# A decoder-trunk kernel on one core: 32x32 diagonal blocks inverted on VectorE, two doubling levels left on TensorE

## The chip, the core and the metric

The kernel runs on one core of a Trainium2 chip. The metric is the device time in microseconds (us) of one execution; lower is better. All tensors are float32.

## What is computed

One layer of a hybrid decoder on 256 tokens of width 1024: a combined projection, a gated-DeltaNet head group (4 heads) and a differential-attention head group (4 heads), their output projection and a layer norm; then cross attention to 256 memory tokens and a layer norm; then a mixture of experts (top 4 of 32) and a last layer norm. The change touches the gated-DeltaNet part alone. The reference solves, per chunk and head, a unit lower triangular system:

```python
lmat = jnp.where(strict, jnp.einsum('bhncd,bhnsd->bhncs', k_beta, k) * decay, 0.0)
amat = lmat + jnp.eye(C)
rhs = jnp.concatenate([v_beta, k_beta * jnp.exp(g)[..., None]], -1)
sol = lax.linalg.triangular_solve(amat, rhs, left_side=True, lower=True, unit_diagonal=True)
```

## The kernel before

It is written out by hand: each engine has its own straight list of instructions, and semaphores order them. The gated-DeltaNet part works on 8 pairs (2 blocks of 128 tokens by 4 heads; `PAIRS`), so there are 8 triangular matrices `I + L` of 128x128. TensorE fills one PSUM bank at a time; each filling is a unit with a name (`dqk0`, `LT0`, `M1_0` ...). The list `UNITS` gives their order, eight banks are used in turn, and column "A" or "D" of the list says whether ScalarE (ACT) or VectorE (DVE) empties the bank. A unit begins when the unit eight places before it has been emptied.

**The inverses.** `X` holds the inverse of each triangular matrix so far and `XT` its transpose, both 128x1024 (8 pairs of 128 columns). Blocks of size 1 are their own inverse, the first level (blocks of 2) is written straight from the mask and `L`: DVE does it for `X` (L1426 and L1428), GpSimd (POOL) for `XT` (L513 and L515) after ACT has emptied `LT0` and `LT1`, the transposes of `L`. Six levels follow (`for level in range(1, LEVELS)`), each of which doubles the block size: POOL masks `LT` into `BT` (L521); TensorE makes `M = BT' X` (L959, units `M{level}_0` and `_1`), ACT empties it (L575), TensorE makes the products for `X` (L964) and for `XT` (L966), and DVE subtracts them (L1471 and L1473). The last level makes `XT` alone.

**What fills the waits.** Behind each level TensorE has other work that depends on nothing in it (`LEVEL_FILL`): `dqk3` behind level 1 (L818), `dv0` behind 2 (L828), `dv1` and four transposes `memT` behind 3 (L828, L810), and behind levels 4, 5 and 6 the scores of differential head 0, 1 or 2 (`sc`, L939) and one quarter of the memory keys (`km`, L818). Behind levels 5 and 6 also `aT`, the transposed attention (L948). The softmax of a head goes DVE `shifted` (L1444 to L1449), ACT `diff_exp` (L660), DVE `combine` (L1455 to L1462), TensorE `attention_T`.

**After the levels** come the products that use the inverse (`U`, `WT`, `S`, `O0`, `WS`, `O1`), head 3 of the differential attention, `vm0`, `OD0`, `OD1`, `vm1`, the mixing projection, cross attention, and the expert loop: 33 rounds, in each of which a block of up to 64 tokens goes through one expert (one of the 32 experts has two blocks). An expert's weights come in six loads of 2 MB. SyncE (SP) issues the weight loads; the buffers hold two experts, and a load waits until TensorE has used the part that it overwrites (L435).

```python
            pool.tensor_tensor(XT, LT, tile_b(levT[0], PAIRS, P), ALU.mult)
            pool.drain()
            pool.tensor_tensor(XT, tile_b(ident, PAIRS, P), XT, ALU.subtract).then_inc(xt_init, 1)
...
            tt(X, L, tile_b(lev0, PAIRS, P), ALU.mult)
            dve.drain()
            tt(X, tile_b(ident, PAIRS, P), X, ALU.subtract).then_inc(x_init, 1)
```

Of the kernel before, what the change touches and what calls it, by code (L numbers as in the profile page):

```python
# [26 lines left out]
P = 128  # L27
# [16 lines left out]
LEVELS = 7  # L44
DIFF_D = 64
# [16 lines left out]
K_ID, K_IOTA, K_UT, K_US, K_ONE, K_CM, K_LEV0, K_LEVT = 0, 128, 192, 320, 448, 576, 960, 1088  # L62
N_CONST = K_LEV0
N_LEVEL_MASKS = P * (LEVELS + 1)
K_END = K_LEV0 + N_LEVEL_MASKS


def constants():

    r = np.arange(P)[:, None]  # L70
    c = np.arange(P)[None, :]
    out = np.zeros((P, K_END), np.float32)
    out[:, K_ID:K_ID + P] = r == c
    out[:, K_UT:K_UT + P] = r <= c
    out[:, K_US:K_US + P] = r < c
    out[:, K_ONE:K_ONE + P] = 1.0
    future = np.where(c > r, NEG, 0.0)
# [7 lines left out]
    out[:, K_LEV0:K_LEV0 + P] = below(r, c, 1)  # L85
    for level in range(LEVELS):
        at = K_LEVT + P * level
        out[:, at:at + P] = below(c, r, 1 << level)
    return out
# [13 lines left out]
def unit_table():  # L103
# [7 lines left out]
    u += [("LT0", "A"), ("LT1", "A"), ("dqk2", "A")]  # L111
# [7 lines left out]
    u += [("U0", "A"), ("U1", "A"), ("WT", "A"), ("sc3_0", "D"), ("sc3_1", "D"), ("S", "A"), ("O0", "A"), ("aT2", "A")]  # L119
    u += [("WS", "D"), ("km3", "A"), ("O1", "A"), ("aT3", "A"), ("vm0", "A"), ("OD0", "A"), ("OD1", "A"), ("vm1", "A")]  # L120
# [54 lines left out]
def trunk_kernel(nc, d, out):  # L175
    ctx = ExitStack()
    with ctx:
# [77 lines left out]
        lev0 = ln_mem[:, 0:P]  # L255
        levT = [ln_mem[:, P * (1 + i):P * (2 + i)] for i in range(LEVELS)]
# [115 lines left out]
        lmat_ready = sem("lmat_ready")  # L372
        x_init = sem("x_init")
# [119 lines left out]
        def _(pool):  # L493
# [15 lines left out]

            wait_emptied(pool, "LT1")  # L510
            wait_emptied(pool, "KQ1")
            pool.wait_ge(ld_lev, 16)
            pool.tensor_tensor(XT, LT, tile_b(levT[0], PAIRS, P), ALU.mult)  # L513
            pool.drain()
            pool.tensor_tensor(XT, tile_b(ident, PAIRS, P), XT, ALU.subtract).then_inc(xt_init, 1)  # L515
            for level in range(1, LEVELS):
                if level == 1:
# [33 lines left out]
        def _(act):  # L551
# [9 lines left out]
            act.dma_start(ln_mem[:, 0:N_LEVEL_MASKS], d["consts"][:, K_LEV0:K_LEV0 + N_LEVEL_MASKS]).then_inc(ld_lev, 16)  # L561
# [73 lines left out]
            empty("dqk2", dqk3[:, 4:6, :], as3(2))  # L635

# [38 lines left out]
            for level in range(1, LEVELS):  # L675
                for g in range(TB):
                    empty(f"M{level}_{g}", M1[:, 4 * g:4 * g + 4, :], as3(4))
                if level == 1:
                    empty("dqk3", dqk3[:, 6:8, :], as3(2))
                elif level <= 3:  # L680
                    empty(f"dv{level - 2}", dv3[:, level - 2, :])
                if level == 3:
                    for i in range(4):
                        empty_T("memT", i, memT)
                if level >= 4:
                    diff_exp(level - 4, 0)
                    diff_exp(level - 4, 1)
                    empty_km(level - 4)
                    if level > 4:
                        empty_aT(level - 5)  # L690
# [4 lines left out]
            empty_head_out("O0", o_flat[:, 0:512], 0, 0, 0)  # L695
            empty_aT(2)
            diff_exp(3, 0)
            diff_exp(3, 1)
            empty_km(3)
            empty_head_out("O1", o_flat[:, 512:1024], 1, 1, 0)  # L700
# [87 lines left out]
        def _(pe):  # L788
# [162 lines left out]

            pe.wait_ge(x_init, 1)
            pe.wait_ge(xt_init, 1)
            for level in range(1, LEVELS):
                pe.wait_ge(bt_ready, level)
                for g in range(TB):
                    if level > 1:
                        need(f"X{level - 1}_{g}", f"XT{level - 1}_{g}")
                    per_head(f"M{level}_{g}", lambda o, h: pe.matmul(o, BT[:, 4 * g + h, :], X[:, 4 * g + h, :],  # L959
                                                                   start=True, stop=True))  # L960
                for g in range(TB):
# [6 lines left out]
                if level == 1:  # L968
                    dqk_unit(3)
                elif level == 2:  # L970
                    arrived(6)
                    dv_unit(0)
                    used_up(2, "dqk3")
                elif level == 3:
                    dv_unit(1)
                    pe.wait_ge(ld_mem, 16)
                    for i in range(4):
                        transpose_block(f"memT{i}", mem3[:, i // 2, :], range(4 * (i % 2), 4 * (i % 2) + 4))
                else:
                    if level == 4:  # L980
                        need("memT3", "dqk3")
                        used_up(1, "dv1")
                        arrived(7)
                        arrived(8)
                    scores(level - 4)
                    km_unit(level - 4)
                    if level > 4:
                        attention_T(level - 5)
# [6 lines left out]
            scores(3)  # L995
# [4 lines left out]
            attention_T(2)  # L1000
            need("WT", "S")
            per_head("WS", lambda o, h: pe.matmul(o, wT[:, h, :], S_sb[:, h, :], start=True, stop=True))
            km_unit(3)
# [5 lines left out]
            last.then_inc(unit_filled, 1)  # L1009
            attention_T(3)  # L1010
# [297 lines left out]
        def _(dve):  # L1308
# [117 lines left out]
            tt(X, L, tile_b(lev0, PAIRS, P), ALU.mult)  # L1426
            dve.drain()
            tt(X, tile_b(ident, PAIRS, P), X, ALU.subtract).then_inc(x_init, 1)  # L1428
            dve.wait_ge(xt_init, 1)
# [36 lines left out]
            for level in range(1, LEVELS):  # L1466
# [8 lines left out]
                if level >= 4:  # L1475
                    if level > 4:
                        combine(level - 5)
                    shifted(level - 4, 0)
                    shifted(level - 4, 1)
# [20 lines left out]
            combine(2)  # L1500
            shifted(3, 0)
            shifted(3, 1)
# [4 lines left out]
            dve.sem_inc(dve_emptied, 1)  # L1507
            combine(3)
# [253 lines left out]
```

## Time and profile before

| what | value |
|---|---|
| median of 3 runs | 1304.68 us (1303.6 to 1306.26) |
| the profiled execution | 1308.02 us |
| its span (first to last instruction) | 1306.3 us |
| mean granted TensorE clock | 0.985 |
| TensorE matmul busy | 1256.5 us (96%) |
| VectorE / ScalarE / GpSimd busy | 331.2 / 282.8 / 46.6 us |
| moved by DMA | 446.83 MB, mean 342 GB/s |

The span is the profiled execution without the 1.7 us that lie around it. A busy engine is not yet the bound: the chain of waits says which work ended last at each point of time, and the timeline says what an engine waited for before an instruction. Times in rows are microseconds from the span's start. PE is TensorE. A full-width fp32 product stands in the rows as two instructions; the built order below counts it as one.

### The profile page before, as it was taken

How to read it: one execution, taken by the hardware profiler on the slowest of the kernel's cores; microseconds unless marked ns; L12 is line 12 of the kernel's file. 1: busy time of each engine (PE TensorE's matmuls, PEld its weight loads, DVE VectorE, ACT ScalarE, POOL GpSimd, SP SyncE). 2: the span in 40 equal slices, each digit the busy share in tenths (PEclk: the TensorE clock that was granted, in tenths of full speed). 3: DMA queues.
4: the chain of work that ended last, by engine and by line, in shares of the span. 5: the costliest groups of instructions: out<-in, count | busy, mean ns of one | idle time of the engine just before them, and what ended most of it. 6: DMA issues, size and time to landing. Idle time of an engine off the chain costs nothing.

```text
span 1306.3 us, 15882 instructions
## 1 busy us (share of the span) xinstructions
PE 1256.5 (96%) x5875; PEld 589.3 (45%) x5876; DVE 331.2 (25%) x935; ACT 282.8 (22%) x501; POOL 46.6 (4%) x39
## 2 busy tenths in 40 slices
PE   7999999999989999999999999999999999998994
PEld 6878796685533333333333333333333333333331
DVE  1652252320421122211222112221112212111115
ACT  0231233111112122121221212212122211221121
POOL 0103101000100000000000000000000000000001
PEclk9999999999889999999999999999999999999998
DMA  8650404058769994999999999999999999999992
GB/s 312 229 208 7 189 1 169 35 227 335 303 264 426 430 427 180 429 427 430 427 430 428 427 429 428 428 429 427 429 428 428 429 428 429 428 428 429 428 429 85
DMA packets 42903, 446.83 MB, mean 342 GB/s; under 512 B 6768, under 2 KB 7104, under 8 KB 18304
## 3 DMA queue, kind: packets, MB, share of 16 engines
q1 hardware_dynamic: 39312, 441.50, 80.5%
q10 hardware_dynamic: 3568, 5.01, 1.2%
q8 instruction: 16, 0.26, 0.1%
q14 instruction: 7, 0.06, 0.0%
HBM read 445.44 MB, written 1.05 MB: 342 GB/s over the span
## 4 chain that ended last, share of the span: by engine, by line
PE 77%; DMA 19%; issue 2%; DVE 1%; POOL 0%; another core or an unknown queue 0%; SPq 0%; POOLq 0%; ACT 0%; DVEq 0%; ACTq 0%
PE bank L1240 28%; DMA main<-in_exp_w_up_dram 19%; PE bank L1283 13%; PE bank L828 8%; PE bank L818 5%; PE bank L1213 3%; PE bank L1181 3%; PE bank L1255 3%; PE bank L1047 2%; PE bank L1187 1%; PE bank L869 1%; PE bank L959 1%; PE bank L966 1%; PE bank L859 1%; PE bank L964 1%
## 5 line engine op out<-in xcount | busy, mean ns | idle before, releaser
L1240 PE MATMUL bank<-main 128*64 128x512 f32 x2112 | 478.4, 604 | 20.9 <-DMA main<-in_exp_w_up_dram 16.3
L1240 PEld LDWEIGHTS bank<-main 128*64 128x64 f32 x2112 | 154.5, 139 | 313.7 <-issue 309.7
L1283 PE MATMUL bank<-main,kst 128*64 128x512 f32 x1056 | 241.1, 598 | 0.0
L1691 DVE TENSOR_TENSOR main<-bank,main 128x256 f32<-128x256 f32 x66 | 28.1, 425 | 588.2 <-PE bank L1255 588.2
L772 ACT ACTIVATE main<-bank 128x512 f32<-128x512 f32 x66 | 39.4, 597 | 430.5 <-PE bank L1240 430.5
L1283 PEld LDWEIGHTS bank<-main,kst 128*64 128x64 f32 x1056 | 69.9, 136 | 122.9 <-issue 118.6
L828 PE MATMUL bank<-main 128*128 128x512 f32 x256 | 111.9, 592 | 0.3 <-ACT main L648 0.3
L818 PE MATMUL bank<-main 128*128 128x256 f32 x352 | 77.9, 380 | 0.0
L828 PEld LDWEIGHTS bank<-main 128*128 128x128 f32 x256 | 47.9, 190 | 56.1 <-issue 55.9
L818 PEld LDWEIGHTS bank<-main 128*128 128x128 f32 x352 | 66.3, 190 | 10.2 <-issue 1.5
L1213 PE MATMUL bank<-main 64*128 64x512 f32 x272 | 67.6, 615 | 0.7 <-ACT main L781 0.7
L575 ACT ACTIVATE main<-bank 128x512 f32<-128x512 f32 (+2 forms) x59 | 33.9, 587 | 155.4 <-PE bank L818 54.9
L1181 PE MATMUL bank<-main,kst 128*64 128x512 f32 x272 | 65.6, 604 | 1.2 <-issue 1.2
L1255 PEld LDWEIGHTS bank<-kst,main 128*128 128x128 f32 x264 | 36.8, 209 | 53.5 <-issue 53.5
L1255 PE MATMUL bank<-kst,main 128*128 128x128 f32 x264 | 49.3, 309 | 0.0
L526 POOL TENSOR_TENSOR small<-small 128x1 f32<-128x1 f32 (+1 forms) x10 | 8.4, 837 | 1101.6 <-DVE small L1717 944.9
L779 ACT ACTIVATE main<-bank 128x256 f32<-128x256 f32 x33 | 12.7, 386 | 151.6 <-PE bank L1292 151.6
L1678 DVE TENSOR_SCALAR main<-kst,small 128x128 f32<-128x128 f32 x66 | 15.9, 284 | 108.4 <-PE bank L1292 105.6
L772 ACT ACT_TABLE_LOAD x33 | 42.3, 1283 | 3.5 <-DVEq L1664 2.9
L781 ACT ACTIVATE main<-bank 128x512 f32<-128x512 f32 x33 | 19.7, 597 | 105.9 <-PE bank L1283 105.9
L777 ACT ACT_TABLE_LOAD x33 | 42.3, 1283 | 0.6
L1181 PEld LDWEIGHTS bank<-main,kst 128*64 128x64 f32 x272 | 19.8, 138 | 40.0 <-issue 40.0
(247 smaller groups left out, 855.1 us busy)
## 6 DMA issues: line engine op xcount, KB each, us to landing
main<-in_exp_w_gate_dram SPq DMA_DIRECT2D x64, 2048.0 KB, 30.1
main<-in_exp_w_up_dram SPq DMA_DIRECT2D x64, 2048.0 KB, 34.5
main<-in_exp_w_down_dram SPq DMA_DIRECT2D x64, 2048.0 KB, 32.9
main<-in_w_in_dram SPq DMA_DIRECT2D x7, 2048.0 KB, 27.8
main<-in_xa_wk_dram SPq DMA_DIRECT2D x2, 2048.0 KB, 10.9
main<-in_w_out_dram SPq DMA_DIRECT2D x2, 2048.0 KB, 11.3
main<-in_xa_wv_dram SPq DMA_DIRECT2D x2, 2048.0 KB, 10.7
main<-in_xa_wq_dram SPq DMA_DIRECT2D x2, 2048.0 KB, 13.2
```

The costliest lines, as they stand in the source:

```text
L575: act.activation(dst, ps[:, :] if src is None else src(ps), func, **kw).then_inc(act_emptied, 1)
L772: act.activation(gu[:, f, :], gu_bank[f][:, :], ACT.Copy).then_inc(gu_copied, 1)
L777: act.activation(sig[:, f, :, :], mg[:, f, :, :], ACT.Sigmoid, scale=SWIGLU_ALPHA).then_inc(sig_ready, 1)
L818: last = pe.matmul(ps[:, j * SEQ:(j + 1) * SEQ], w(k)[:, c * P:(c + 1) * P], src[:, k, :], start=(k == 0), stop=(k == KC - 1))
L828: last = pe.matmul(ps[:, :], srcT[:, k, b * P:(b + 1) * P], w(k)[:, col:col + 512], start=(k == 0), stop=(k == KC - 1))
L1047: last = pe.matmul(ps[:, j * SEQ + b * P:j * SEQ + (b + 1) * P], w(k)[:, (2 * i + j) * P:(2 * i + j + 1) * P], xT[:, k, b * P:(b + 1) * P] ...
L1181: last = pe.matmul(ps[64 * h:64 * h + 64, :], selw[:, b, 0:CAP], x3[:, b, h * HALF:(h + 1) * HALF], start=(b == 0), stop=(b == 1))
L1213: last = pe.matmul(acc[b][h][:, :], gselT[64 * h:64 * h + 64, b * P:(b + 1) * P], y_sb[64 * h:64 * h + 64, :], start=False, stop=final)
L1240: last = pe.matmul(gu_bank[f][64 * side:64 * side + 64, :], xg_chunk(k), weights(role, k, f), start=(k == 0), stop=(k == KC - 1))
L1255: last = pe.transpose(guT_bank[f][:, j * P:(j + 1) * P], gu[:, f, :].rearrange("p (c j) -> p j c", j=4)[:, j, :], ident)
L1283: last = pe.matmul(y_bank[64 * h:64 * h + 64, :], hT[:, k, :], weights(role, k, h), start=(k == 0), stop=(k == KC - 1))
L1691: tt(mg[:, f, :, :], gT[:, :, 0, :], bias(0), ALU.add)
```

## The change

Levels 1 to 4 and the two masked first steps go. In their place the 32 diagonal blocks of 32x32 (4 in each of the 8 pairs) are inverted together on DVE. POOL writes `diag`, the diagonal blocks of `I - L`, in four instructions of 32 partitions each. A DVE transpose in 32x32 blocks spreads them over the partitions as `factor`: a partition then holds one whole block and solves 8 of its 32 columns, so four partitions share a block. Row `r` of the inverse is a product of `r + 1` factors with 8 columns of the rows so far, summed: one multiply and one reduction, 31 times, each waiting for the one before. Two transposes and two masked copies then write `X` and `XT`. TensorE goes on at level 5. The fillings are placed anew: `dqk3`, `dv0` and `memT` ahead of level 5, the scores and `dv1` behind it, head 1, `km0` and `aT0` behind level 6, and the rest (`km1`, `km2`, heads 2 and 3) among the products that use the inverse. The load of the masks shrinks from 1024 to 516 columns.

```diff
+FIRST_LEVEL = 5
...
 LEVEL_FILL = {
-    1: [("dqk3", "A")],
-    2: [("dv0", "A")],
-    3: [("dv1", "A")] + [(f"memT{i}", "A") for i in range(4)],
-    4: [("sc0_0", "D"), ("sc0_1", "D"), ("km0", "A")],
-    5: [("sc1_0", "D"), ("sc1_1", "D"), ("km1", "A"), ("aT0", "A")],
-    6: [("sc2_0", "D"), ("sc2_1", "D"), ("km2", "A"), ("aT1", "A")],
+    5: [("sc0_0", "D"), ("sc0_1", "D"), ("dv1", "A")],
+    6: [("sc1_0", "D"), ("sc1_1", "D"), ("km0", "A"), ("aT0", "A")],
 }
...
+            pool.wait_ge(lmat_ready, 2)
+            pool.wait_ge(unit_filled, UNIT_AT["ktok1"] + 1)
+            for q in range(4):
+                rows = slice(32 * q, 32 * q + 32)
+                pool.drain()
+                last = pool.tensor_tensor(diag[rows, :, :], ident[rows, rows].unsqueeze(1).broadcast_to([32, PAIRS, 32]),
+                                          L[rows, :, rows], ALU.subtract)
+            last.then_inc(diag_ready, 1)
...
+            dve.wait_ge(diag_ready, 1)
+            dve.transpose(factor, diag.rearrange("p g k -> p k g").unsqueeze(3).broadcast_to([P, 32, PAIRS, 4]))
+            dve.drain()
+            for r in range(1, 32):
+                done = solved[:, 0:r + 1, :].rearrange("p k j -> p j k")
+                product = products[:, 0:8 * (r + 1)].rearrange("p (j k) -> p j k", j=8)
+                tt(product, factor[:, 0:r + 1, r].unsqueeze(1).broadcast_to([P, 8, r + 1]), done, ALU.mult)
+                dve.drain()
+                dve.reduce_sum(solved[:, r, :], product, AX_X)
+                dve.drain()
...
+            dve.transpose(diag_X.rearrange("p g (d j) -> p j g d", j=8), solved.rearrange("p r j -> p j r"))
+            dve.drain()
+            spread(X, diag_X).then_inc(x_init, 1)
+            dve.transpose(diag_XT, diag_X)
+            dve.drain()
+            spread(XT, diag_XT).then_inc(xt_init, 1)
...
-            for level in range(1, LEVELS):
+            for level in range(FIRST_LEVEL, LEVELS):
                 for g in range(TB):
                     empty(f"M{level}_{g}", M1[:, 4 * g:4 * g + 4, :], as3(4))
...
+                if level == FIRST_LEVEL:
+                    empty("dv1", dv3[:, 1, :])
+                    diff_exp(0, 0)
+                    diff_exp(0, 1)
+                else:
+                    empty_km(0)
+                    empty_aT(0)
+                    diff_exp(1, 0)
+                    diff_exp(1, 1)
```

TensorE's queue from the filling ahead of the first level on, before (the names in these rows are regions of memory: `main` is SBUF, `kst` the constants, `bank` PSUM):

```order
L818 MATMUL bank<-main 128x256 x16
L959 MATMUL bank<-main 128x128 x8
L964 MATMUL bank<-main 128x128 x4
L966 MATMUL bank<-main 128x128 x4
L964 MATMUL bank<-main 128x128 x4
L966 MATMUL bank<-main 128x128 x4
L818 MATMUL bank<-main 128x256 x16
L959 MATMUL bank<-main 128x128 x8
```

And now, from `dqk2` and `dqk3` on (L836 here is L818 before, L846 is L828, L828 is L810, L984, L990 and L992 are L959, L964 and L966):

```order
L836 MATMUL bank<-main 128x256 x32
L846 MATMUL bank<-main 128x512 x8
L828 MATMUL bank<-kst,main 128x128 x16
L984 MATMUL bank<-main 128x128 x8
L990 MATMUL bank<-main 128x128 x4
L992 MATMUL bank<-main 128x128 x4
L990 MATMUL bank<-main 128x128 x4
L992 MATMUL bank<-main 128x128 x4
L957 MATMUL bank<-main 128x128 x2
L957 MATMUL bank<-main 128x256 x2
L846 MATMUL bank<-main 128x512 x8
L984 MATMUL bank<-main 128x128 x8
```

Three fillings now stand in one piece ahead of the first level, and behind level 5 only the scores and `dv1` stand ahead of the `M` of level 6.

ACT's queue, before, at the end of level 4 and in level 5 (behind the last of `memT` come `M4_0` and `M4_1`, the exponentials of head 0, then `km0`, `M5_0`, `M5_1`):

```order
L648 ACTIVATE main<-bank 128x4x128 x4
L575 ACTIVATE main<-bank 128x512 x2
L660 ACTIVATE main,small<-main,small 128x128
L660 ACTIVATE main,small<-main,small 128x256
L660 ACTIVATE main,small<-main,small 128x128
L660 ACTIVATE main,small<-main,small 128x256
L575 ACTIVATE main<-bank 128x512 x3
```

And now (L663 is L648 before, L588 is L575, L675 is L660; the three behind `memT` are `M5_0`, `M5_1` and `dv1`, the three behind the exponentials `M6_0`, `M6_1` and `km0`):

```order
L663 ACTIVATE main<-bank 128x4x128 x4
L588 ACTIVATE main<-bank 128x512 x3
L675 ACTIVATE main,small<-main,small 128x128
L675 ACTIVATE main,small<-main,small 128x256
L675 ACTIVATE main,small<-main,small 128x128
L675 ACTIVATE main,small<-main,small 128x256
L588 ACTIVATE main<-bank 128x512 x3
```

The exponentials of head 0 stood ahead of the emptying of the filling behind their level; they now stand behind it, directly ahead of `M6_0`.

## Rows read from the trace of the kernel before

**Rows 1.** The page: TensorE's busy time, and the chain's shares by engine.
```profile
PE 1256.5 (96%) x5875; PEld 589.3 (45%) x5876; DVE 331.2 (25%) x935; ACT 282.8 (22%) x501; POOL 46.6 (4%) x39
...
PE 77%; DMA 19%; issue 2%; DVE 1%; POOL 0%; another core or an unknown queue 0%; SPq 0%; POOLq 0%; ACT 0%; DVEq 0%; ACTq 0%
```

**Rows 2.** The chain of waits, 110 to 150 us: start us, us, what.
```profile
110.85 2.02 PE bank L959 x16
112.87 0.95 PE bank L964 x8
113.82 0.89 PE bank L966 x8
...
123.41 1.78 PE bank L959 x16
...
147.98 1.75 PE bank L810 x16
```

**Rows 3.** SP's queue in the timeline: start us, us from first to last issue.
```profile
472.08 4.29 SPq L435 DMA_DIRECT2D main<-in_exp_w_down_dram  x2
510.16 0.34 SPq L435 DMA_DIRECT2D main<-in_exp_w_gate_dram  x1
```

**Rows 4.** Busy time by stretch; the last three columns: granted clock, DMA share, GB/s.
```profile
363.00:366.00 3.00, 2.77 (x8) 0.93 (x10) 1.23 (x6) 0.05 (x1) 0.00 (x0) 0.50 0.02 5
...
495.00:500.00 5.00, 5.00 (x26) 1.89 (x27) 1.70 (x5) 0.39 (x1) 0.00 (x0) 1.00 0.00 0
```

**Rows 5.** PE's timeline, 93 to 111 us: start us, us, work, idle before.
```profile
93.80 1.04 PE L926 MATMUL bank<-kst,main 128*128 128x128 f32 x8
...
102.45 7.07 PE L818 MATMUL bank<-main 128*128 128x256 f32 x32
110.85 1.35 PE L959 MATMUL bank<-main 128*128 128x128 f32 x10 [1.32 <-POOL main L521]
```

**Rows 6.** DVE's timeline, 352 us on: small instructions, each after a drain.
```profile
352.00 0.23 DVE L1617 TENSOR_TENSOR small<-small 128x64 f32<-128x64 f32 x1
352.30 0.22 DVE L1619 TENSOR_REDUCE small<-small 128x2 f32<-128x64 f32 x1
```

**Rows 7.** One group by line: count, then busy us and mean ns.
```profile
L1343 DVE COPY main<-small 128x1024 f32<-128x1024 f32 x1 | 0.7, 696 | 0.1
```

**Rows 8.** Timeline of DVE and POOL, 97 to 111 us.
```profile
98.46 1.23 DVE L1428 TENSOR_TENSOR main<-kst,main 128x1024 f32<-128x1024 f32 x1
108.39 2.21 DVE L1433 TENSOR_TENSOR small<-small 128x1 f32<-128x1 f32 x1 [8.71 <-POOL main L515]
...
103.44 2.35 POOL L513 TENSOR_TENSOR main<-main 128x1024 f32<-128x1024 f32 x1 [12.42 <-ACT main L575]
105.93 2.35 POOL L515 TENSOR_TENSOR main<-kst,main 128x1024 f32<-128x1024 f32 x1
108.24 2.35 POOL L521 TENSOR_TENSOR main<-main 128x1024 f32<-128x1024 f32 x1
```

**Rows 9.** ACT's timeline: an emptying ahead of another, and one head's exponentials.
```profile
148.02 0.60 ACT L575 ACTIVATE main<-bank 128x512 f32<-128x512 f32 x1 [9.90 <-PE bank L828]
148.51 2.06 ACT L648 ACTIVATE main<-bank 128x512 f32<-128x512 f32 x4
...
196.15 0.44 ACT L660 ACTIVATE main<-main,small 128x128 f32<-128x128 f32 x1
...
197.81 0.22 ACT L660 ACTIVATION_READ_ACCUMULATOR main<-main,small 128x1 f32 x1
```

**Rows 10.** The chain: eight transposes of dense columns, four of every fourth column.
```profile
243.75 0.87 PE bank L810 x8
...
406.71 0.68 PE bank L1255 x4
```

**Rows 11.** The chain: the first and the third round's weight products.
```profile
363.23 15.02 PE bank L1240 x56
...
421.79 12.02 PE bank L1240 x56
```

More of the change, by code:

```diff
@@ L110, in unit_table @@
     u += [("KK0", "D"), ("KK1", "D"), ("KQ0", "D"), ("KQ1", "D"), ("ktok0", "D"), ("ktok1", "D"), ("dqk1", "A")]
-    u += [("LT0", "A"), ("LT1", "A"), ("dqk2", "A")]
-    for level in range(1, LEVELS):
+    u += [("LT0", "A"), ("LT1", "A"), ("dqk2", "A"), ("dqk3", "A"), ("dv0", "A")] + [(f"memT{i}", "A") for i in range(4)]
+    for level in range(FIRST_LEVEL, LEVELS):
         u += [(f"M{level}_0", "A"), (f"M{level}_1", "A")]
@@ L254, in trunk_kernel @@
         iota = kst[:, K_IOTA:K_IOTA + CAP]
-        lev0 = ln_mem[:, 0:P]
-        levT = [ln_mem[:, P * (1 + i):P * (2 + i)] for i in range(LEVELS)]
+        levT = {level: ln_mem[:, S_LEVT + P * i:S_LEVT + P * (i + 1)] for i, level in enumerate(range(FIRST_LEVEL, LEVELS))}
+        block_mask = ln_mem[:, S_BLOCK:S_BLOCK + 4]
+        solved = ln_mem[:, S_EYE:S_EYE + 256].rearrange("p (r j) -> p r j", j=8)
+        factor = conv_out[:, 0:1024].rearrange("p (k r) -> p k r", k=32)
+        products = conv_out[:, 1024:1280]
+        diag, diag_X, diag_XT = (conv_out[:, 256 * i:256 * (i + 1)].rearrange("p (g c) -> p g c", g=PAIRS) for i in (5, 6, 7))
         ln_g, ln_b = ln_mem[:, 0:D_MODEL], ln_mem[:, D_MODEL:2 * D_MODEL]
@@ L635, in _ @@
             empty("dqk2", dqk3[:, 4:6, :], as3(2))
+            empty("dqk3", dqk3[:, 6:8, :], as3(2))
+            empty("dv0", dv3[:, 0, :])
             def empty_km(i):
@@ L949, in attention_T @@
                 last.then_inc(unit_filled, 1)
+            dqk_unit(3)
+            arrived(6)
+            dv_unit(0)
+            used_up(2, "dqk3")
+            pe.wait_ge(ld_mem, 16)
+            for i in range(4):
+                transpose_block(f"memT{i}", mem3[:, i // 2, :], range(4 * (i % 2), 4 * (i % 2) + 4))
             pe.wait_ge(x_init, 1)
-            pe.wait_ge(xt_init, 1)
-            for level in range(1, LEVELS):
-                pe.wait_ge(bt_ready, level)
+            for level in range(FIRST_LEVEL, LEVELS):
+                pe.wait_ge(bt_ready, level - FIRST_LEVEL + 1)
                 for g in range(TB):
-                    if level > 1:
+                    if level > FIRST_LEVEL:
                         need(f"X{level - 1}_{g}", f"XT{level - 1}_{g}")
@@ L967, in _ @@
                                                                     start=True, stop=True))
[L968 to L974, printed above, removed]
+                if level == FIRST_LEVEL:
+                    need("dqk3")
+                    scores(0)
                     dv_unit(1)
-                    pe.wait_ge(ld_mem, 16)
-                    for i in range(4):
-                        transpose_block(f"memT{i}", mem3[:, i // 2, :], range(4 * (i % 2), 4 * (i % 2) + 4))
-                else:
[L980 to L988, printed above, removed]
+                else:
+                    scores(1)
+                    need("memT3")
+                    arrived(7)
+                    arrived(8)
+                    km_unit(0)
+                    attention_T(0)
+                    used_up(1, "dv1")
             for g in range(TB):
@@ L994, in _ @@
             per_head("WT", lambda o, h: pe.matmul(o, kbg[:, 4 + h, :], XT[:, 4 + h, :], start=True, stop=True))
-            scores(3)
+            scores(2)
             need("U0")
@@ L1464, in combine @@
                 last.then_inc(a_ready, 1)
-            for level in range(1, LEVELS):
+            for level in range(FIRST_LEVEL, LEVELS):
                 for g in range(TB):
@@ L1474, in _ @@
                 dve.drain()
[L1475 to L1479, printed above, removed]
+                if level > FIRST_LEVEL:
+                    combine(0)
+                shifted(level - FIRST_LEVEL, 0)
+                shifted(level - FIRST_LEVEL, 1)
             roots = [0]
@@ L1507, in _ @@
             dve.sem_inc(dve_emptied, 1)
+            combine(2)
+            shifted(3, 0)
+            shifted(3, 1)
             combine(3)
```

78 lines of the change are left out of this document (39 added, 39 removed).

## The prediction

> **What bounds the kernel now.** First the page: TensorE is busy for 96% of the span, but the chain gives it 77% and gives 19% to DMA [rows 1], so two stretches with different bounds must be told apart. The chain in order of time does that. From 110.85 us on it steps from one TensorE group straight to the next through all six levels [rows 2]; there the time is TensorE's, and a product taken away is time gained, as long as nothing else comes late. DMA ends the chain in the last quarter, in the expert loop. So the second question is whether a gain made at 110 us survives the loads. SP's queue answers it. In the round in which one expert has a second block, SP issues its last load at about 476 us and the next at 510.16 [rows 3], and the engines moved nothing between 495 and 500 us [rows 4]. That pause ends when TensorE frees a buffer. Before it, DMA stood idle at 363 to 366 us [rows 4], again until TensorE frees the first one. The load stream behind each pause therefore starts at a time that TensorE sets. All of it moves when TensorE is earlier, and the end with it. I pass the gain on in full.
>
> **What goes from TensorE.** A level is one group of `M` and four of `X`, `XT`: in level 1, 2.02 + 0.95 + 3 x 0.89 = 5.64 us, in level 2 with 1.78 in front 5.40 us, in levels 3 and 4 the same within 0.01 [rows 2]. Four levels: 5.64 + 3 x 5.40 = 21.84 us. The first `M` after a wait costs 2.02 instead of 1.78, and that now falls on level 5: -0.24. The old wait ahead of level 1, 1.32 us for POOL's `XT` and `BT`, goes [rows 5]: +1.32. With no new wait the gain would be 22.9 us. The other units are all still there, only moved.
>
> **What now has to be ready, and when.** TensorE starts `dqk2` at 102.45 us [rows 5], as before. Behind it stand `dqk3` (a unit like it), `dv0` and `memT`. `dqk2` and `dqk3` take 6.9 us each, `memT` 1.75 [rows 2], `dv0`, eight 512-column products, also 6.9 as its work is that of `dqk2`. TensorE is through at about 102.45 + 3 x 6.9 + 1.75 = 124.9 us. The question is whether `X` is written by then.
>
> *POOL's `diag`.* It may begin when the transposes of `k` are done, 93.80 + 1.04 = 94.84 us [rows 5]. A POOL product of 1024 columns takes 2.35 us, and 0.14 lies between two with a drain (105.93 - 103.44 - 2.35) [rows 8]. A quarter of the columns: 0.59 + 0.14 = 0.73 us, four times 2.9 us, so 97.9 us. Bounds: POOL's fixed part is not in a row, so from no more than 0.59 to twice that an instruction, +2.4 us.
>
> *The first transpose.* No row has one. A copy of 1024 columns took 0.70 us [rows 7], a two-input product 1.23 [rows 8], a POOL instruction 2.35 [rows 8]. It is one pass over 1024 columns without the copy's fast form, so I take 1.23, and 0.07 for the drain: 99.2 us. Bounds -0.5 and +1.1 us.
>
> *The 31 steps.* A drained two-input product of 64 columns starts 0.30 us ahead of the next instruction and takes 0.23 of them; a reduction of 64 takes 0.22, so I price it alike [rows 6]. The product of 1024 takes 1.23 [rows 8]. A line through 0.23 at 64 and 1.23 at 1024 has 1.04 ns a column and 0.16 us fixed; with 0.07 of drain a step's instruction costs 0.23 us plus 1.04 ns a column. There are 62 instructions. Their columns are 8(r + 1) for r = 1 to 31, 8 x 527 = 4216, in the product and again in the reduction, 8432 in all. Sum: 62 x 0.225 + 8432 x 0.00104 = 14.0 + 8.8 = 22.7 us. Bounds: the fixed part within 0.03, +-1.9 us; the column price is the subject of a rival.
>
> *POOL in between.* `BT` for level 5 is now POOL's first instruction after `LT1` is emptied, so it falls at 103.4 us, in the middle of the steps. The small DVE product at 108.39 us took 2.21 us for one column and ended with the POOL instruction that had begun at 108.24 [rows 8]: a DVE product with two SBUF inputs waits for a POOL product. That costs the steps about 2.2 us once. `BT` itself is early.
>
> *The way back.* A transpose of 256 columns, by the same line 0.43 + 0.07 = 0.5 us, and the masked copy of 1024, 1.23 us [rows 8]. `X` is ready at 99.2 + 22.7 + 2.2 + 0.5 + 1.2 = 125.8, seen by TensorE at about 126.0 us. `XT` follows 0.5 + 1.2 us later, at 127.7; TensorE needs it only after the `M` of level 5, at 126.0 + 2.0 = 128.0. So one wait, 126.0 - 124.9 = 1.1 us.
>
> **The new wait in ACT's queue.** This one comes from the order alone. Before, the exponentials of a head stood ahead of the emptying of a 7 us filling and had ended long before the next `M`. Now head 0's four stand behind the emptying of `dv1`, and `M6_0` behind them. When `dv1` is filled, ACT empties it (the next instruction may start 0.49 us after it) [rows 9], then spends 197.81 - 196.15 + 0.22 = 1.9 us on the exponentials [rows 9], then empties `M6_0` in 0.60 [rows 9]: 3.0 us. TensorE needs that bank after `M6_0` and `M6_1`, 1.8 us. It waits 1.2 us. I looked for the same at the other places. Behind level 6, the emptying of `U0` stands behind `km0`, `aT0` and head 1's exponentials, about 3 us; TensorE has `aT0`, `U0`, `U1`, `WT` and the scores to do before it needs `U0`, 3.9 us at 0.89 a group of 8 [rows 2]. Ahead of `aT1` lie these and `S` and `O0`, 5.7 us, against 1.9 us of exponentials, 1.0 of emptying and about 1.9 of `combine` (an estimate from its columns by the line above). `aT2` and `aT3` have a `km` of 6.9 us ahead of them. These places cost nothing, with under 1 us to spare at the first two.
>
> **The sum.** 21.84 - 0.24 + 1.32 - 1.1 - 1.2 = 20.6 us. Against the profiled execution: span 1306.3 - 20.6 = 1285.7, execution 1308.0 - 20.6 = 1287.4. That execution stands 3.3 us above the median of the runs, so for the median: 1304.7 - 20.6 = **1284.1 us**.
>
> **Where the column price could be wrong.** Both inputs of each product are read with a stride: `factor` 128 bytes, `solved` 32 bytes from one column to the next. No DVE row has that. A TensorE row does: eight transposes of dense columns take 0.87 us, four that take every fourth column (16 bytes apart) 0.68, that is 0.170 for 0.109 each, 1.56 times [rows 10]. I keep the dense price, since DVE asks for a column every 1.04 ns and TensorE's dense transposes for one every 0.85; by TensorE's strided 1.33 ns a column it would be +1.2 us, by the ratio 4216 x 1.04 x 0.56 = +2.5 us.
>
> The Trainium skill ("SBUF — State Buffer", "Door 1: The DMA port swizzle") says that SBUF is read in lines of 16 bytes and that an access which goes to a new line each time pays a penalty, at least two hits per line being needed to hide the latency. The TensorE row agrees; no DVE row of this case shows it. Against it the same skill ("VectorE: DVE Perf Modes", "Mode 1x (REGULAR) — the baseline") says that the mode fp32 products run in makes no assumption on strides.
>
> **The rivals.**
>
> *Strided reads at half speed.* The products pay 2.08 ns a column: +4.4 us, the wait ahead of level 5 becomes 5.5 us. TensorE's clock may fall on that: after 3.4 us of light work and idling the granted clock was 0.50 at 363 us [rows 4], and the first round's weight products took 15.02 us for 12.02 two rounds on [rows 11], 3.0 us. Against that, the 1.32 us wait left the clock alone. Time: 1288.5, with the clock 1291.5. Chance 0.18.
>
> *The inverse is hidden.* Steps at 0.20 us fixed (-1.6) or a transpose at copy speed (-0.5) take the 1.1 us wait away; without ACT's wait too the gain is 22.9. Time 1281.8 to 1283. Chance 0.11.
>
> *The loads take it back.* If some stretch of loads between 205 and 510 us were the bound, the expert loop would start earlier and end at the same time: 1304.7. The two pauses [rows 3, 4] speak against it. Chance 0.03.
>
> *Slower.* The change puts 62 dependent instructions where TensorE has nothing else left. If one of them costs 0.56 us instead of 0.23 and its columns, the steps grow by 62 x 0.33 = 20.6 us and the gain is gone; at 0.60 us with the 3.0 us of clock the kernel takes 1284.1 + 62 x 0.37 + 3.0 = 1310. The drained rows at 0.30 us for 64 columns [rows 6] speak against it. Chance 0.03.
>
> **How the numbers follow.** The forecast keeps 0.65. Its range: all waits gone at the lower end, 1304.7 - 22.9 = 1281.8, less a little for the runs' own spread, 1281.5; at the upper end the bounds of POOL (2.4), the transpose (1.1), the steps (1.9) and the stride (2.5) do not all fall together; the root of the sum of their squares is 4.1, which gives 1288.2, and the stride rival with its clock reaches 1291.5. I take 1281.5 to 1292. A measurement of this kernel tells 0.2%, 2.6 us, from no change. Faster by more: 0.65 + 0.18 + 0.11 = 0.94; the same 0.03; slower 0.03.
>
> **What would show it.** In the changed profile: the 62 small DVE instructions end about 22.7 + 2.2 us after they start, and the growth from one product to the next is 8 x 1.04 ns; the `X` copy ends near 125.8 us; TensorE idles 1.1 us ahead of level 5 for DVE and 1.2 us ahead of level 6's `XT` for ACT, and nowhere else between 100 and 200 us; the first round of the expert loop starts at 342.6 instead of 363.23 us [rows 11]; SP's pause ends at 489.6 instead of 510.16 [rows 3]. It would be wrong if the wait ahead of level 5 is over 5 us (column or instruction price), if the clock there falls, or if the first round is 20 us earlier and the end is not (loads).

## The result, and the profile after

| | before | changed |
|---|---|---|
| median (4 runs each) | 1304.66 us (1303.6 to 1306.26) | 1290.72 us (1290.14 to 1293.29) |
| profiled execution / its span | 1308.02 / 1306.3 us | 1290.89 / 1288.7 us |
| VectorE busy | 331.2 us | 343.7 us |
| TensorE matmul busy | 1256.5 us | 1228.4 us |

The ratio is 0.9892, 95% interval [0.9877, 0.9907]: 13.9 us faster, clear of the 0.2% that a measurement can tell. The forecast was 20.6 us and 1284.1 us; the gain is two thirds of that. The time lies inside the range, near the "strided reads" rival with its clock (1291.5), for which the range had been drawn that wide.

The page's first line and its chain by engine, after the change:

```profile
PE 1228.4 (95%) x5683; PEld 565.3 (44%) x5684; DVE 343.7 (27%) x984; ACT 276.8 (21%) x493; POOL 35.3 (3%) x37
...
PE 73%; DMA 16%; DVE 5%; DVEq 2%; issue 2%; SPq 1%; another core or an unknown queue 1%; POOLq 0%; ACT 0%; POOL 0%; ACTq 0%
```

VectorE has 5% of the chain, against 1% [rows 1]. Where, the TensorE timeline of the changed kernel tells (start us, us, work, idle before). It answers to [rows 2, 5]:

```profile
123.16 1.91 PE L828 MATMUL bank<-kst,main 128*128 128x128 f32 x16
130.42 3.78 PE L984 MATMUL bank<-main 128*128 128x128 f32 x16 [5.35 <-DVE main L1459]
133.99 1.91 PE L990 MATMUL bank<-main 128*128 128x128 f32 x8
135.69 1.30 PE L992 MATMUL bank<-main 128*128 128x128 f32 x8
136.83 1.06 PE L990 MATMUL bank<-main 128*128 128x128 f32 x8
...
146.54 1.95 PE L984 MATMUL bank<-main 128*128 128x128 f32 x16
149.66 2.02 PE L992 MATMUL bank<-main 128*128 128x128 f32 x16 [1.18 <-issue]
```

Three things are to be seen. `memT` starts at 123.16 us and ends at 125.0, as forecast (124.9). Then TensorE waits 5.35 us for `X` where 1.1 was forecast. And the `M` of level 5 take 3.78 us where those of level 6 take 1.95: the busy time by stretch (granted clock third from the end) has TensorE at 1.2 GHz there.

```profile
130.40:134.00 3.60, 3.58 (x17) 3.59 (x18) 1.85 (x4) 0.60 (x1) 0.00 (x0) 0.50 0.00 0
134.00:137.00 3.00, 3.00 (x19) 3.00 (x19) 0.69 (x1) 0.60 (x1) 2.37 (x1) 0.64 0.00 0
```

The last row of the timeline is the wait in ACT's queue at level 6: 1.18 us, forecast 1.2.

The DVE timeline of the changed kernel shows the chain that TensorE waits for:

```profile
98.52 1.25 DVE L1448 STREAM_TRANSPOSE main<-main 128x1024 f32<-128x1024 f32 x1 [1.26 <-POOL main L522]
99.85 0.18 DVE L1453 TENSOR_TENSOR main<-main 128x16 f32<-128x16 f32 x1
100.10 0.17 DVE L1455 TENSOR_REDUCE main<-main 128x8 f32<-128x16 f32 x1
...
103.83 2.12 DVE L1453 TENSOR_TENSOR main<-main 128x72 f32<-128x72 f32 x1
...
127.21 0.63 DVE L1453 TENSOR_TENSOR main<-main 128x256 f32<-128x256 f32 x1
127.91 0.42 DVE L1455 TENSOR_REDUCE main<-main 128x8 f32<-128x256 f32 x1
128.40 0.66 DVE L1462 STREAM_TRANSPOSE main<-main 128x256 f32<-128x256 f32 x1
129.14 1.23 DVE L1459 TENSOR_TENSOR main<-main 128x1024 f32<-128x1024 f32 x1
```

The reduction of 256 columns is on the line that [rows 6, 8] gave, 0.43. The product of 256 takes 0.63, 0.20 more, and the one of 16 takes 0.18: the excess grows with the columns. The steps take 128.40 - 99.85 = 28.55 us against 24.9 forecast with POOL's part. Up to their start the sum is 0.65 us short (99.85 for 99.2); in the steps it is 3.65 us short.

**Where the gain shows.** The chain has the first products of the output projection at 222.91 us in the kernel before and at 209.56 in the changed one:

```profile
222.91 20.84 PE bank L828 x48
```

```profile
209.56 20.84 PE bank L846 x48
```

`dqk2` starts at 102.48 us, before at 102.45 [rows 5]. That stretch is 13.4 us shorter, and the median 13.9. The spans of the two profiles differ by more, 17.6 us; the run `before_again` below says why.

### The profile page after: what moved, and what is told of

It reads as the page before. It is cut to its first block, busy times and chain, and to the rows that moved or that the text cites. A ratio compares the mean times of both kernels' runs of the same rounds, so it can differ in the third digit from the quotient of the medians.

```text
span 1288.7 us, 15582 instructions
## 1 busy us (share of the span) xinstructions
PE 1228.4 (95%) x5683; PEld 565.3 (44%) x5684; DVE 343.7 (27%) x984; ACT 276.8 (21%) x493; POOL 35.3 (3%) x37
## 4 chain that ended last, share of the span: by engine, by line
PE 73%; DMA 16%; DVE 5%; DVEq 2%; issue 2%; SPq 1%; another core or an unknown queue 1%; POOLq 0%; ACT 0%; POOL 0%; ACTq 0%
PE bank L1261 29%; DMA main<-in_exp_w_up_dram 15%; PE bank L1304 14%; PE bank L846 8%; PE bank L836 4%; PE bank L1202 3%; PE bank L1276 3%; PE bank L1068 2%; DVEq L1733 1%; DVE main L1453 1%; PE bank L887 1%; DVE kst L1741 1%; DVE main L1737 1%; PE bank L1313 1%; DVE main L1455 1%
## 5 line engine op out<-in xcount | busy, mean ns | idle before, releaser
L1261 PE MATMUL bank<-main 128*64 128x512 f32 x2112 | 470.8, 596 | 23.4 <-DMA main<-in_exp_w_up_dram 20.1
L1261 PEld LDWEIGHTS bank<-main 128*64 128x64 f32 x2112 | 151.7, 137 | 311.2 <-issue 307.2
L846 PE MATMUL bank<-main 128*128 128x512 f32 x256 | 112.1, 593 | 0.3 <-ACT main L663 0.3
L836 PE MATMUL bank<-main 128*128 128x256 f32 x352 | 77.7, 380 | 0.0
L846 PEld LDWEIGHTS bank<-main 128*128 128x128 f32 x256 | 48.0, 190 | 56.7 <-issue 56.5
L836 PEld LDWEIGHTS bank<-main 128*128 128x128 f32 x352 | 66.4, 190 | 9.9 <-issue 0.8
L588 ACT ACTIVATE main<-bank 128x512 f32<-128x512 f32 (+2 forms) x51 | 28.6, 583 | 165.7 <-PE bank L836 65.5
L797 ACT ACTIVATE main<-bank 128x256 f32<-128x256 f32 x33 | 12.7, 385 | 155.7 <-PE bank L1313 155.7
```

Of the source, the lines that this page charges most:

```text
L588: act.activation(dst, ps[:, :] if src is None else src(ps), func, **kw).then_inc(act_emptied, 1)
L836: last = pe.matmul(ps[:, j * SEQ:(j + 1) * SEQ], w(k)[:, c * P:(c + 1) * P], src[:, k, :], start=(k == 0), stop=(k == KC - 1))
L846: last = pe.matmul(ps[:, :], srcT[:, k, b * P:(b + 1) * P], w(k)[:, col:col + 512], start=(k == 0), stop=(k == KC - 1))
L1261: last = pe.matmul(gu_bank[f][64 * side:64 * side + 64, :], xg_chunk(k), weights(role, k, f), start=(k == 0), stop=(k == KC - 1))
```

## The experiments

All start from the changed kernel but for `before_again`. The profiled executions start `dqk2` up to 4 us apart, so the stretch from the first `memT` transpose to the first product of the output projection is compared too; where `dv1` stands ahead of it, its 6.87 us are added.

| run | stretch, us | wait ahead of level 5 | `M` of level 5 | median, us | ratio to before, interval |
|---|---|---|---|---|---|
| changed kernel, first | 86.40 | 5.35 | 3.78 | 1290.72 | 0.9892 [0.9877, 0.9907] |
| `after_again` | 85.22 | 5.36 | 3.60 | 1290.27 | 0.9881 [0.9866, 0.9897] |
| `dense` | 81.20 | 2.82 | 2.05 | 1287.56 | 0.9858 [0.9833, 0.9883] |
| `warm` | 83.78 | filled | 2.02 | 1290.53 | 0.9866 [0.9837, 0.9895] |
| `act_order` | 85.00 | 5.34 | 3.78 | 1291.51 | 0.9875 [0.9847, 0.9903] |
| `cover` | 76.79 | none | 1.95 | 1283.27 | 0.9821 [0.9798, 0.9845] |
| `pad` | 85.34 | 5.35 | 3.74 | 1289.70 | 0.9881 [0.9866, 0.9896] |
| `best` | 76.79 | none | 1.95 | 1282.31 | 0.9829 [0.9815, 0.9842] |
| `best_pad` | 76.78 | none | 1.95 | 1282.34 | 0.9823 [0.981, 0.9837] |

The kernel before stood at 1306.78 us beside `dense` to `cover`, and at 1305.52 beside the last three and `after_again`; times of different groups are compared by their ratios. `factor_dense`, `solved_dense`, `act_bt` and `before_again` were executed once each (1293.18, 1293.51, 1289.85 and 1302.85 us), beside one execution of the kernel before at 1302.48. They are read by their profiles alone.

### `dense`: the columns of both inputs of the products side by side

```diff
-        factor = conv_out[:, 0:1024].rearrange("p (k r) -> p k r", k=32)
+        factor = conv_out[:, 0:1024].rearrange("p (r k) -> p k r", k=32)
-        solved = ln_mem[:, S_EYE:S_EYE + 256].rearrange("p (r j) -> p r j", j=8)
+        solved = ln_mem[:, S_EYE:S_EYE + 256].rearrange("p (j r) -> p r j", j=8)
```

The part of the constants that `solved` starts from is laid out to match; that hunk is left out here.

> Both inputs of the 31 products are laid out so that neighbouring columns lie side by side (the first transpose writes with a stride instead, the last one reads dense); nothing else. Theory (the stride costs the products 0.83 ns a column, 3.5 us in all): the product of 256 columns takes 0.42 to 0.43 us instead of 0.63, the steps take 25 us instead of 28.6, X is ready near 127 us, TensorE's wait ahead of level 5 falls from 5.35 to about 1.8 us and the granted clock stays 1.00, as behind the 1.32 us wait of the kernel before. Time: 1290.7 - 3.5 - 2.7 = 1284.5 us. Rival (a product of this form, with a broadcast input, costs that much whatever its stride): products unchanged, 1290.7 us. Second rival: the strided write moves the cost to the transpose, which then takes 2 us or more for 1.25, and a part of the 3.5 us is given back.

Groups by line and form of `dense` (busy us, mean ns after the bar), then its TensorE timeline:

```profile
L1448 DVE STREAM_TRANSPOSE main<-main 128x1024 f32<-128x1024 f32 x1 | 1.9, 1946 | 1.2 <-POOL main L522 1.2
...
L1453 DVE TENSOR_TENSOR main<-main 128x256 f32<-128x256 f32 x1 | 0.4, 425 | 0.1
L1455 DVE TENSOR_REDUCE main<-main 128x8 f32<-128x256 f32 x1 | 0.4, 422 | 0.1
```

```profile
124.96 1.91 PE L828 MATMUL bank<-kst,main 128*128 128x128 f32 x16
129.69 2.05 PE L984 MATMUL bank<-main 128*128 128x128 f32 x16 [2.82 <-DVE main L1459]
```

The product of 256 columns takes 425 ns instead of 626, the same as the reduction. The 31 products sum to 11.21 us for 14.46. The strides cost 3.25 us, 0.77 ns a column. Of that the first transpose, which now writes with a stride, takes 0.70 back (1.95 for 1.25 us), as the second rival had it. The wait falls to 2.82 us and the clock behind it stays at 1.00. The stretch is 4.0 to 5.2 us shorter. The wait was expected at 1.8 us and the time at 1284.5; it is 1287.56, and by the ratios the gain over the changed kernel is 4.4 us for the 6.2 expected. The transpose's 0.70 us and the 0.25 that the strides cost less than expected are most of what the wait has too much.

### `factor_dense` and `solved_dense`: one input at a time

Each has one of the two lines of the diff above, `solved_dense` with the matching constants.

> Only factor is laid out so that its columns lie side by side; solved keeps its 32 byte stride. Theory (any input that goes to another 16 byte line with each column holds the product up, and the two are read at the same time, so one strided input is enough): the product of 256 columns stays at 0.6 us or more. Rival (each strided input adds its own share): it takes about 0.52 us, half way between 0.63 and 0.425. Second rival (the 128 byte stride of factor is the one that costs): 0.43 us.

> Only solved is laid out side by side; factor keeps its 128 byte stride, and the first transpose its dense output. Theory (one strided input is enough): the product of 256 columns stays at 0.6 us or more. Rival (shares): about 0.52 us. Second rival (factor's stride is the one): 0.63; then the other run shows 0.43. The first transpose takes 1.25 us, against 1.95 with the strided output: that the difference is the output's alone is seen here.

The row of the product of 256 columns, first with only `factor` dense, then with only `solved` dense:

```profile
L1453 DVE TENSOR_TENSOR main<-main 128x256 f32<-128x256 f32 x1 | 0.6, 617 | 0.1
```

```profile
L1453 DVE TENSOR_TENSOR main<-main 128x256 f32<-128x256 f32 x1 | 0.6, 582 | 0.1
```

With both strided it was 626, with none 425. One strided input is enough for 157 to 192 of the 201 ns; the shares do not add. The first transpose takes 1.25 us with `factor` written dense and 1.95 with it strided, in both runs, so that difference is the output's. `factor_dense` alone makes TensorE wait longer than the changed kernel does, 5.90 us for 5.35, since it pays 0.70 us for the transpose and gains 9 ns on the widest product; `solved_dense`, which pays nothing, waits 4.79. Their single times (1293.18 and 1293.51 us) do not tell them apart.

### `warm`: no idling, the same wait

```diff
+            ps = begin(f"M{FIRST_LEVEL}_0")
+            for _ in range(25):
+                pe.matmul(ps[:, 0:P], ident, ident, start=True, stop=True)
             pe.wait_ge(x_init, 1)
```

> 25 products of the identity with itself, of 128 columns, stand on TensorE ahead of its wait for X and write a bank that level 5 overwrites; nothing else. They take 25 x 0.22 = 5.5 us and cover the 5.35 us of idling without ending it. Theory (the idling lets the clock fall, and level 5's first groups ran at half of it for 2.7 us more): the granted clock stays 1.00 behind the wait, the 16 instructions of M take 1.8 to 2.0 us instead of 3.78, time 1288 us. Rival (the groups were slow for another reason, such as reading X just after it is written): M takes 3.78 us again and the time stays at 1290.7 us or grows by 0.2.

```profile
127.11 5.75 PE L980 MATMUL bank<-kst 128*128 128x128 f32 x50
132.70 2.02 PE L987 MATMUL bank<-main 128*128 128x128 f32 x16
134.56 1.13 PE L993 MATMUL bank<-main 128*128 128x128 f32 x8
```

The TensorE timeline has the products up to the moment when `X` is there, and the `M` behind them at full speed: the idling made the groups slow, not what they read. The stretch is 2.6 us shorter than in the first profile of the changed kernel and 1.4 shorter than in `after_again`, where the clock had come back sooner. The median of four runs, 1290.5 for the 1288 expected, does not show it; by the ratio it is 0.9866 for 0.9892, and the intervals overlap.

### `act_order`: the exponentials ahead of the emptying of `dv1`

```diff
-                    empty("dv1", dv3[:, 1, :])
                     diff_exp(0, 0)
                     diff_exp(0, 1)
+                    empty("dv1", dv3[:, 1, :])
```

> ACT does head 0's four exponentials ahead of the emptying of dv1, not behind it; nothing else. Theory (M6_0 waits in ACT's queue behind them): TensorE's 1.18 us wait ahead of level 6's XT goes, time 1289.5 us. Rival (the wait is DVE's or the bank's): the wait stays, 1290.7 us.

```profile
148.33 1.95 PE L984 MATMUL bank<-main 128*128 128x128 f32 x16
150.12 2.02 PE L992 MATMUL bank<-main 128*128 128x128 f32 x16
```

No idle time stands ahead of `XT` any more: the wait was ACT's queue. The microsecond is in the trace; the medians cannot tell it (1291.5 with a kernel before at 1306.8).

### `act_bt`: no POOL product during the steps

```diff
-                    wait_emptied(pool, "vtok1")
...
+            wait_emptied(pool, "vtok1")
+            pool.memset(BT, 0.0).then_inc(bt_zero, 1)
...
+            for at0 in (0, 64):
+                last = act.activation(BT[at0:at0 + 32, :, at0 + 32:at0 + 64], LT[at0:at0 + 32, :, at0 + 32:at0 + 64], ACT.Copy)
+            last.then_inc(bt_ready, 1)
```

> BT of level 5 is no longer POOL's masked product of 1024 columns: POOL fills it with zeros, and ACT copies into it the two blocks of 32 rows that are not zero. Theory (a DVE product waits for a POOL product): the one product of 2.12 us at 104 us takes its 0.29, the steps end 1.8 us earlier, and TensorE's wait ahead of level 5 falls from 5.35 to about 3.5 us; whether the clock falls behind a wait of that length is open (it stayed behind 2.82). Rival (the long product is something of its own at that place, such as the fetching of instructions): one product of about 2 us is still there. The filling with zeros may itself hold a product up by up to 1 us.

```profile
104.47 0.28 DVE L1458 TENSOR_TENSOR main<-main 128x64 f32<-128x64 f32 x1
105.11 0.29 DVE L1458 TENSOR_TENSOR main<-main 128x72 f32<-128x72 f32 x1
```

The product of 72 columns takes 0.29 us; in the changed kernel it took 2.12 and ended with POOL's product, which began at 103.45 and took 2.35. POOL's filling with zeros (99.81 to 100.76 us) fell on the first transpose, which took its 1.25 us as ever; what it would do to a product no run shows. TensorE's wait falls to 3.56 us and the stretch to 83.63:

```profile
129.90 2.86 PE L989 MATMUL bank<-main 128*128 128x128 f32 x16 [3.56 <-DVE main L1464]
```

The `M` of level 5 begin at full clock here (0.97 up to 131.0 us) and then fall to 0.50 until about 134.4: the 3.56 us of idling still cost clock, the 2.82 of `dense` did not.

### `cover`: `dv1` ahead of level 5, `km0` and `km1` behind levels 5 and 6

```diff
-    5: [("sc0_0", "D"), ("sc0_1", "D"), ("dv1", "A")],
-    6: [("sc1_0", "D"), ("sc1_1", "D"), ("km0", "A"), ("aT0", "A")],
+    5: [("sc0_0", "D"), ("sc0_1", "D"), ("km0", "A")],
+    6: [("sc1_0", "D"), ("sc1_1", "D"), ("km1", "A"), ("aT0", "A")],
...
             used_up(2, "dqk3")
+            dv_unit(1)
             pe.wait_ge(ld_mem, 16)
...
                     diff_exp(0, 0)
                     diff_exp(0, 1)
+                    empty_km(0)
                 else:
-                    empty_km(0)
-                    empty_aT(0)
                     diff_exp(1, 0)
                     diff_exp(1, 1)
+                    empty_km(1)
+                    empty_aT(0)
```

The first lines place the units, the middle ones are TensorE's list, the last ones ACT's, where the exponentials of both heads also move ahead of the emptyings of `km0` and `km1`.

> dv1, 6.9 us of TensorE work, stands ahead of level 5 instead of behind it, km0 moves behind level 5 and km1 behind level 6, with the exponentials of heads 0 and 1 ahead of the emptyings of km0 and km1 on ACT; the chain on DVE is untouched. Theory (the loss against the forecast is one wait that TensorE has nothing for, and the clock behind it): TensorE is through at 131.9 us, X at 130.4, no wait, clock 1.00, and the 1.18 us at level 6 go as well: 1290.7 - 5.35 - 2.7 - 1.2 = 1281.5 us. Rival (what is taken from the wait comes back behind it, since U, S and aT1 now have less work between them): 1285 us or more, with new waits between 160 and 190 us.

```profile
129.90 1.91 PE L828 MATMUL bank<-kst,main 128*128 128x128 f32 x16
131.65 1.95 PE L985 MATMUL bank<-main 128*128 128x128 f32 x16
...
145.04 1.95 PE L985 MATMUL bank<-main 128*128 128x128 f32 x16
146.83 2.02 PE L993 MATMUL bank<-main 128*128 128x128 f32 x16
```

No wait ahead of level 5, none at level 6, and none in the timeline up to the output projection. The stretch is 9.6 us shorter than in the first profile, forecast 9.3, and it comes out at the end: 1283.27 us, 23.5 below the kernel before on that chip. (The 1281.5 expected was reckoned from the changed kernel's first median, beside which the kernel before stood 2.1 us lower; by the ratios `cover` gains 9.3 us on the changed kernel.) From 102.35 us, where its TensorE row with `dqk2` begins, to 199.82 `cover` takes 97.5 us, the kernel before 120.5: 23.0 us, where the prediction's sum without new waits was 22.9.

### `best`, `after_again`, `pad`, `best_pad`

`best` is `cover` with both layouts of `dense`. `pad` and `best_pad` keep the rows of the constants as wide as before:

```diff
-K_END = K_SOLVE + N_SOLVE
+K_END = K_SOLVE + 1024
```

> The order of the run with dv1 ahead of level 5, and both inputs of the products side by side. Theory (with dv1 ahead, TensorE is through 1.2 us or more after X is there, so DVE's steps are off the path): X is ready 3 us earlier and nothing is gained by it, the time stands where that run stood, 23 us below the kernel before. Rival (the shorter steps bring another microsecond or more, through a wait not seen): 25 us below.

> The changed kernel, unchanged, beside the next three on one chip. Expected 14 us below the kernel before, as measured first. TensorE's wait ahead of level 5 is 5.35 us again, the M of level 5 take 3.78 us and the wait at level 6 is 1.18 us; the small load that TensorE waits for at 12 us lands later than in the kernel before, as in all seven profiles of changed kernels so far (TensorE began the beta and decay columns at 13.0 to 14.2 us, in the two profiles of the kernel before at 12.4 and 12.7).

> The changed kernel, with the rows of the constants in memory as wide as before (1984 columns, the last 508 unused and not loaded); the loads move the same data. Theory (the late small load comes from the changed length or start of the rows that the two loads of constants read): TensorE begins the beta and decay columns at 12.4 to 12.7 us as in the kernel before, and the time falls by 0.6 to 1.8 us. Rival (it comes from the smaller load itself, or from the code, or is chance): 13 us or more again and the same time.

> The run before it with the wide rows of constants. Theory: lowest of all, below it by what the wide rows brought the changed kernel (0.6 to 1.8 us), about 24 us below the kernel before. Rival (the wide rows bring nothing): the same time as without them.

`after_again` repeats the wait (5.36 us) and the gain (ratio 0.9881), while its `M` of level 5 take 3.60 us for 3.78. `best` has the stretch of `cover` to 0.01 us, 76.79, though its chain should be some 2.5 us shorter by `dense` (products 3.25 us less, first transpose 0.70 more): once TensorE has work up to then, DVE's speed is worth nothing. `best` and `cover` cannot be told apart in their ratios, and both beat the two kernels.

The wide rows do what was expected in the profile and nothing that the times can tell. The TensorE row of the beta and decay columns, in `after_again` and then in `pad`:

```profile
14.21 6.97 PE L868 MATMUL bank<-dnw_keep,main 128*128 128x8 f32 x32 [2.44 <-DMA small<-in_gdn_dt_bias_dram]
```

```profile
12.39 4.90 PE L868 MATMUL bank<-dnw_keep,main 128*128 128x8 f32 x32 [0.83 <-DVE main L1340]
```

In all ten profiles with narrow rows this row waits for DMA and starts at 13.0 to 14.2 us; in the four with wide ones (`pad`, `best_pad` and the kernel before twice) it starts at 12.4 to 12.7 and waits for DVE. The medians are 1289.7 for 1290.3 and 1282.3 for 1282.3. Whether executions without a profile have that wait stays open.

### `before_again`: a second profile of the kernel before

> The kernel before, unchanged, for a second profile. Its first profiled execution stood 3.3 us above the median, and from its first weight round on the gain in the profiles was 16.6 us, where it had been 13.4 us up to the router. Theory (the granted clock between the router and the first round, where TensorE has little work, differs from execution to execution by some 3 us): that stretch, from the start of the router products to the first weight products, takes another time here than 24.4 us, and the stretch from level 1 to vm0 takes the same 93.6 us within 0.1. Rival (the changed kernel gains the 3 us there by its own doing, through the loads): both stretches take the same as before, within 0.3 us.

The TensorE rows of the router's end and of the first weight products, in the first profile and in the second:

```profile
341.87 2.91 PE L1145 MATMUL bank<-kst 128*128 128x128 f32 x12
...
354.85 3.36 PE L1181 MATMUL bank<-main,kst 128*64 128x512 f32 x8 [1.22 <-issue]
```

```profile
340.93 1.58 PE L1145 MATMUL bank<-kst 128*128 128x128 f32 x12
...
352.42 1.94 PE L1181 MATMUL bank<-main,kst 128*64 128x512 f32 x8 [1.22 <-issue]
...
359.38 14.40 PE L1240 MATMUL bank<-main 128*64 128x512 f32 x56 [3.39 <-issue]
```

The same 12 products took 2.91 us once and 1.58 the other time. The granted clock was 0.83 from 338.8 to 348.8 us in the first profile and 1.00 over the same work in the second. From the transposes directly ahead of the router products (338.81 and 338.02 us) to the first weight products it is 24.4 us in one execution, 21.4 in the other, and 21.2 in the changed kernel; from level 1 to `vm0` the chain takes 93.64 us in both of the kernel before. The span was 1301.1 us. So of the 3.7 us by which the two first profiles differ beyond 13.9, 3.2 lie in this stretch; they are TensorE's clock in one execution of the kernel before, and no part of the change.

## Why the prediction was right, and where it was not

**TensorE as the bound, and the pass-through: right.** `cover` takes every new wait away and comes out 23.0 us shorter in the stretch, 22.9 by the sum of the four levels. The end moves with it: the changed kernel's 13.4 us in the stretch are 13.9 in the median, `cover`'s 23.0 are 23.5. In the changed kernel the first round starts at 346.67 us and SP's first issue behind its pause stands at 492.60, 17.56 before that of [rows 3]: the stretch's 13.4, the 3.2 of the clock near the router, and 1.0 behind it, of which 0.5 is the first round's weight products (14.48 us for 15.02 [rows 11]). The spans end 17.6 us apart. The loads give nothing back.

**The wait in ACT's queue: right.** 1.2 forecast, 1.18 measured, gone in `act_order`.

**POOL in between: right.** 2.2 forecast, 2.12 - 0.29 = 1.83 measured (`act_bt`).

**The column price of the products: the step that failed.** "I keep the dense price" chose the wrong row. TensorE's strided row [rows 10] stood for the stride and I weighed it down by an argument on request rates, which no row had tested. The product pays 1.87 ns a strided column, (626 - 177) / 240, for 1.04, or 1.8 times where TensorE's row has 1.56; 3.25 us in all, above the 2.5 us that I had as its bound, and under the 4.4 of the rival. The Trainium skill's rule on lines of 16 bytes ("SBUF — State Buffer", "Door 1: The DMA port swizzle") has a penalty for going to a new line with each access. The traces agree with a penalty: 582 to 626 ns at strides of 32 and 128 bytes for 425 at 4. No run has a stride inside a line, so none shows how long a line is. The Trainium skill's sentence in "VectorE: DVE Perf Modes" ("Mode 1× (REGULAR) — the baseline"), that this mode makes no assumption on strides, holds for whether it works, not for what it costs.

**The rest of the chain.** `diag` was 0.5 us late (four instructions from 95.10 to 98.41; forecast 97.9, though its own terms, 94.84 + 4 x 0.73, give 97.8), and the first transpose took 1.25 (forecast 1.23). The transpose of 256 columns ahead of `X` took 0.66 us instead of 0.43; the one for `XT` has the same size and no stride:

```profile
130.28 0.43 DVE L1465 STREAM_TRANSPOSE main<-main 128x256 f32<-128x256 f32 x1
```

With its input read dense (`dense`) the first of the two still took 0.64, so it is its strided output. One idle gap of 0.44 us stands between the product of 112 columns and its reduction, in every profile with these steps, and no run explains it. The fixed part and the drains of the 62 instructions come to some 0.4 us more than forecast. POOL's part took 0.4 less. With the stride these make `X` ready at 130.4 instead of 125.8 us.

**The clock: in the rival, not in the sum.** I let it fall only if the wait grew. It grew: 2.8 us lost in the first profile (1.76 in `M`, 0.78 and 0.24 in the two groups behind), none with the idling filled. Together: 20.6 - 4.2 (longer wait) - 2.8 (clock) = 13.6, measured 13.4. The mechanisms were the forecast's; the outcome was that of the rival to which I gave 0.18. That it came so near the rival's numbers (a wait of 5.35 us for 5.5, a time of 1290.7 for 1291.5) is in part luck: the stride cost 3.25 us and not 4.4, and the small terms above, which the sum did not have, made up the rest.

## What to carry to other kernels

Work moved from TensorE to a serial chain on another engine is worth what TensorE has to do meanwhile: count that cover in microseconds, and put one more filling ahead of the wait rather than behind it when the chain's price is uncertain; here 6.9 us of cover, with the new order on ACT (some 1.2 us of it), were worth 8.4 to 9.6 us and the faster chain nothing on top. Lay out the operands that a small instruction reads 31 times so that their columns are neighbours, both of them, since one strided input keeps most of the price, and pay for a stride once, in the transpose that writes it. When fillings are moved, read each queue behind the moved piece again: an emptying that waits for a long filling holds up all that is queued behind it.

## What the runs showed of the hardware

A DVE product of two SBUF inputs in fp32 took 626 ns for 256 columns with strides of 128 and 32 bytes, 617 and 582 with one of them alone, and 425 with none. A DVE transpose of 1024 columns in 32x32 blocks took 1.25 us written dense and 1.95 us written with a stride of 128 bytes; one of 256 columns took 0.43 and 0.64 to 0.66 (stride 32 bytes). A DVE product of two SBUF inputs that fell on a POOL product took 2.12 us for 0.29, while the reduction of 64 columns that fell on it (103.54 us) took its 0.22. Behind 2.82 us of idling TensorE's clock was granted in full; behind 3.56 us it was full for the first microsecond of work and then half for some 3 us; behind 5.35 us it ran at half from the start, for 3.3 to 5.8 us in four profiles. The same wait filled with products of no use kept it. The same light stretch near the router took 21.4 and 24.4 us in two executions of one kernel, with a granted clock of 1.00 and 0.83 over the same first products.
